# Two row halves as one 128-column stationary for the second half of each expert's w1

## The reference, cut to what matters

```python
def run_block(args):
    xblk, e = args
    hid = jax.nn.silu(xblk @ w1[e]) * (xblk @ w3[e])
    return hid @ w2[e]
...
y = jnp.zeros((T + 1, D), jnp.float32).at[slot_tok].add(yb.astype(jnp.float32) * slot_w[:, None])[:T]
```

## Time and profile before

| | |
|---|---|
| median of 3 runs | 1729.02 us (1728.03 to 3334.2) |
| profiled execution | 1730.86 us, its span 1729.0 us |
| PE matmul busy | 1625.4 us, 94% of the span |
| VectorE busy | 1100.1 us, 64% |
| ScalarE busy | 879.8 us, 51% |
| GpSimd busy | 631.2 us, 37% |
| DMA | 340.98 MB, mean 197 GB/s |
| mean granted clock | 0.976 |

### The profile page before, as it was taken

The page is one execution under the profiler, slowest core; times in us unless marked ns, Lnnn a source line. Parts: engine busy times, 40 slices in busy tenths (PEclk is TensorE's granted clock), DMA queues, the critical chain, the costliest instruction groups (busy, mean ns, idle before and its releaser), DMA issues.

```text
span 1729.0 us, 22131 instructions
## 1 busy us (share of the span) xinstructions
PE 1625.4 (94%) x7116; PEld 1220.4 (71%) x7116; DVE 1100.1 (64%) x1449; ACT 879.8 (51%) x1241; POOL 631.2 (37%) x373
## 2 busy tenths in 40 slices
PE   3899999999999999999989998995999999999996
PEld 3788888777878788778878887683666665665654
DVE  6776865371422448433576543336999999999986
ACT  4544533433222333234455334433877877877775
POOL 0578886333324335324464433110122222222221
PEclk9999999999999999999998999996999999999998
DMA  9343444143121153532223221256999999999993
GB/s 324 103 116 111 138 151 160 55 146 103 50 104 49 49 219 134 195 122 93 98 69 109 74 98 49 56 204 251 379 403 405 398 407 400 398 388 377 391 389 123
DMA packets 135424, 340.98 MB, mean 197 GB/s; under 512 B 14596, under 2 KB 66060, under 8 KB 110521
## 3 DMA queue, kind: packets, MB, share of 16 engines
q1 hardware_dynamic: 127938, 320.71, 49.8%
q0 software_dynamic: 5200, 8.41, 2.2%
q10 hardware_dynamic: 2215, 10.93, 1.6%
HBM read 329.78 MB, written 18.87 MB: 202 GB/s over the span
## 4 chain that ended last, share of the span: by engine, by line
PE 61%; DMA 17%; DVE 12%; issue 6%; ACT 3%; DVEq 1%; SPq 0%; POOLq 0%; ACTq 0%; POOL 0%
PE ps L768 17%; PE ps L769 17%; PE ps L770 17%; DMA ring<-in_w 16%; PE ps L740 5%; DVE parts L2388 3%; PE ps L750 2%; DVE act_parts L2388 2%; PE ps L1128 1%; DVE arena L2431 1%; PE ps L1015 1%; DMA ring<-in_w_ada 1%; DVE arena L2447 1%; DVE arena L2081 1%; ACT parts L1226 1%
## 5 line engine op out<-in xcount | busy, mean ns | idle before, releaser
L2502 POOL TENSOR_TENSOR parts<-ring,parts 128x1024 fp32r<-128x1024 f32 x172 | 426.0, 2482 | 620.2 <-ACT parts L1226 617.0
L1226 ACT CAST parts<-ring 128x1024 fp32r<-128x1024 f32 x174 | 180.5, 1048 | 363.3 <-PE ps L770 327.7
L768 PE MATMUL ps<-parts,act_parts 128*128 128x512 f32 (+2 forms) x832 | 327.4, 394 | 7.5 <-DVEq L1909 3.0
L769 PE MATMUL ps<-parts,act_parts 128*128 128x512 f32 (+2 forms) x832 | 322.5, 388 | 0.0
L770 PE MATMUL ps<-parts,act_parts 128*128 128x512 f32 (+2 forms) x832 | 322.4, 387 | 0.0
L768 PE MATMUL ps<-act_parts,parts 128*128 128x512 f32 x640 | 252.0, 394 | 5.0 <-DVEq L1814 5.0
L769 PE MATMUL ps<-act_parts,parts 128*128 128x512 f32 x640 | 249.7, 390 | 0.0
L770 PE MATMUL ps<-act_parts,parts 128*128 128x512 f32 x640 | 249.5, 390 | 0.0
L768 PEld LDWEIGHTS ps<-parts,act_parts 128*128 128x128 f32 (+1 forms) x832 | 150.4, 181 | 72.8 <-issue 32.5
L1601 ACT CAST parts<-ring 128x1024 fp32r<-128x1024 f32 x144 | 144.7, 1048 | 75.7 <-PE ps L770 70.2
L770 PEld LDWEIGHTS ps<-parts,act_parts 128*128 128x128 f32 (+1 forms) x832 | 150.3, 181 | 39.3
(11 more groups left out here) (295 smaller groups left out, 2502.8 us busy)
## 6 DMA issues: line engine op xcount, KB each, us to landing
arena<-in_w SPq DMA_DIRECT2D x96, 1024.0 KB, 13.2
ring<-in_w SPq DMA_DIRECT2D x96, 1024.0 KB, 14.8
ring<-in_w_in SPq DMA_DIRECT2D x30, 1024.0 KB, 7.3
ring<-in_w_in SPq DMA_DIRECT2D x34, 512.0 KB, 5.2
ring<-in_w_ada SPq DMA_DIRECT2D x12, 1024.0 KB, 10.4
ring<-in_w_ret_out SPq DMA_DIRECT2D x8, 1024.0 KB, 6.3
ring<-in_w_out SPq DMA_DIRECT2D x8, 1024.0 KB, 7.6
ring<-in_w_in SPq DMA_DIRECT2D x16, 256.0 KB, 4.1
```

The lines of the kernel that those rows point to most:

```text
L768: pe.matmul(o, lhs[1], rhs[0], start=start, stop=False)
L769: pe.matmul(o, lhs[0], rhs[1], start=False, stop=False)
L1226: act.copy(parts[:, g % 4, 0, :], ring[:, st.place(j), k * 1024:(k + 1) * 1024]).then_inc(dense_hi, 1)
L2502: pool.tensor_tensor(parts[:, g % 4, 1, :], ring[:, st.place(j), k * 1024:(k + 1) * 1024], parts[:, g % 4, 0, :].bitcast(F32), ALU.subtrac ...
```

## The change

Pieces 2 and 3 of w1 are multiplied as w3's are: `xgT[:, t]` with its 128 columns, two products in place of three. Bank 1 then has two row halves. So that all its 128 partitions are begun, the fp32 product of the first half starts with its fourth K tile as a stationary operand of 128 columns whose last 64 are zero (`last_rows`); the zeros are a fifth tile behind `xg_rows`, set once in the routing stage. ScalarE copies the low row half (`low_gate`), VectorE adds it to the high one in `silu_rows` and writes the sum to `t_h`, waits for its own result and releases bank 1; ScalarE applies Silu to `t_h` in place (`gate`), after the cast of piece 8; `hidden` waits for `silu_ready`. Two instructions that set a semaphore without waiters (`x_ready`) are removed.

```diff
@@ allocation and the routing stage
-        xg_rows = carve([KT // 2, SLOTS])
+        xg_rows = carve([KT // 2 + 1, SLOTS])
+        last_rows = xg_rows[:, KT // 2 - 1:, :].rearrange("p t n -> p (t n)")
...
+            own(dve.memset(xg_rows[:, KT // 2, :], 0.0))
@@ PE, up
-                for t in range(KT // 2):
-                    mm = pe.matmul(o[0:SLOTS, :], xg_rows[:, t, :], w1[:, t * FF:(t + 1) * FF], start=t == 0, stop=False)
+                t = KT // 2 - 1
+                pe.matmul(o, last_rows, w1[:, t * FF:(t + 1) * FF], start=True, stop=False)
+                for t in range(KT // 2 - 1):
+                    mm = pe.matmul(o[0:SLOTS, :], xg_rows[:, t, :], w1[:, t * FF:(t + 1) * FF], start=False, stop=False)
...
-                        if n < 4:
-                            mm = split_product(o[0:SLOTS, :], [xgT[:, t, h, :] for h in range(2)], [w[:, h, half] for h in range(2)],
-                                               t == 0, t == KT - 1)
-                        else:
-                            rows = xgT[:, t].rearrange("p h s -> p (h s)")
-                            pe.matmul(o, rows, w[:, 0, half], start=t == 0, stop=False)
-                            mm = pe.matmul(o, rows, w[:, 1, half], start=False, stop=t == KT - 1)
+                        rows = xgT[:, t].rearrange("p h s -> p (h s)")
+                        pe.matmul(o, rows, w[:, 0, half], start=t == 0, stop=False)
+                        mm = pe.matmul(o, rows, w[:, 1, half], start=False, stop=t == KT - 1)
@@ ScalarE
-            def gate(stage, i=0):
-                drained(stage, 1, act.activation(t_h[0:SLOTS, :], full(stage, 1, i)[0:SLOTS, :], ACT.Silu))
+            def low_gate(stage, i=0):
+                act.copy(up_low[0:SLOTS, :], full(stage, 1, i)[SLOTS:2 * SLOTS, :]).then_inc(up_low_ready, 1)
+
+            def gate(b):
+                act.wait_ge(gate_sum_ready, b + 1)
+                act.activation(t_h[0:SLOTS, :], t_h[0:SLOTS, :], ACT.Silu).then_inc(silu_ready, 1)
...
-                gate("moe", i)
+                low_gate("moe", i)
                 high(8, i, 1 - odd)
+                gate(b)
@@ VectorE
+            def silu_rows(stage, b, i=0):
+
+                dve.wait_ge(up_low_ready, b * 2 + 1)
+                ins = dve.tensor_tensor(t_h[0:SLOTS, :], full(stage, 1, i)[0:SLOTS, :], up_low[0:SLOTS, :], ALU.add)
+                ins.then_inc(gate_sum_ready, 1)
+                dve.wait_ge(gate_sum_ready, b + 1)
+                drained(stage, 1, dve.nop())
...
-                dve.wait_ge(bank_drained[st.place(1)], st.before(1, i) + 1)
+                dve.wait_ge(silu_ready, b + 1)
...
                     for n in (6, 7, 8, 9, 10, 11):
                         low(n, r * 20 + (14 + 10 * q + n), q if n < 8 else 1 - q)
+                        if n == 7:
+                            silu_rows("moe", b, r * 2 + (1 + q))
```

More of the change, by code:

```diff
@@ L446, in build @@
             "gates_stored", "gates_in", "gates_used", "merged_ready"))
-        ms_ready, rms_ready, x_ready = (sem(n) for n in ("ms_ready", "rms_ready", "x_ready"))
+        ms_ready, rms_ready = (sem(n) for n in ("ms_ready", "rms_ready"))
         x_rms_ready, in2_r_ready = sem("x_rms_ready"), sem("in2_r_ready")
@@ L475, in build @@
         conv_stored, conv_back = sem("conv_stored"), sem("conv_back")
-        block_w_ready, slot_w_ready, idx_out_ready = sem("block_w_ready"), sem("slot_w_ready"), sem("idx_out_ready")
+        block_w_ready, idx_out_ready = sem("block_w_ready"), sem("idx_out_ready")
         settled = sem("settled")
+        gate_sum_ready, silu_ready = sem("gate_sum_ready"), sem("silu_ready")
         out_done = sem("out_done")
@@ L1620, in high_rows @@
                 o = full(stage, k, i)
-                act.copy(xg_rows, o[:, 0:KT // 2 * SLOTS].rearrange("p (t n) -> p t n", t=KT // 2)).then_inc(xg_rows_ready, 1)
+                act.copy(xg_rows[:, 0:KT // 2, :], o[:, 0:KT // 2 * SLOTS].rearrange("p (t n) -> p t n", t=KT // 2)).then_inc(xg_rows_ready, 1)
                 act.copy(xgT[:, :, 0, :], o.rearrange("p (t n) -> p t n", t=KT)).then_inc(xgT_hi, 1)
-            def gate(stage, i=0):
-                drained(stage, 1, act.activation(t_h[0:SLOTS, :], full(stage, 1, i)[0:SLOTS, :], ACT.Silu))
+            def low_gate(stage, i=0):
[3 more added lines that the diff above has]
+                act.activation(t_h[0:SLOTS, :], t_h[0:SLOTS, :], ACT.Silu).then_inc(silu_ready, 1)
             def low_up(stage, i=0):
@@ L1638, in _ @@
             high(7, 0, 0, used=(up_used, 1))
-            gate("moe_first")
+            low_gate("moe_first")
+            gate(0)
             low_up("moe_first")
@@ L2016, in _ @@
                 dve.tensor_tensor(x[:, m, :], x[:, m, :] if m else x0_early, y_tok[:, m, :], ALU.add).then_inc(row_ready, 1)
-            dve.nop().then_inc(x_ready, 1)
             low_T("h2T", 6, TAPS + 3)
@@ L2436, in add_rows @@
                 dve.nop().then_inc(y_sum_ready, 1)
+            def silu_rows(stage, b, i=0):
[4 more added lines that the diff above has]
+                drained(stage, 1, dve.nop())
             def hidden(stage, b, i=0):
-                dve.wait_ge(up_low_ready, b + 1)
+                dve.wait_ge(up_low_ready, b * 2 + 2)
                 moe(dve.tensor_tensor(up_sum[0:SLOTS, :], full(stage, 2, i)[0:SLOTS, :], up_low[0:SLOTS, :], ALU.add))
@@ L2443, in hidden @@
                 drained(stage, 2, dve.nop())
-                st = banks[stage]
-                dve.wait_ge(bank_drained[st.place(1)], st.before(1, i) + 1)
+                dve.wait_ge(silu_ready, b + 1)
                 w = slot_w[0:SLOTS, b:b + 1] if isinstance(b, int) else slot_w[0:SLOTS, bass.ds(b, 1)]
@@ L2460, in _ @@
             drained("route", 7, dve.nop())
+            silu_rows("moe_first", 0)
             hidden("moe_first", 0)
@@ L2467, in _ @@
                 low(n, 4 + n, 1)
+            silu_rows("moe", 1)
             for n in (8, 9, 10, 11):
```

## The result

The changed kernel takes **1758.78 us** (median of 4 runs, 1756.79 to 1765.85) against 1729.73 us of the kernel before, run beside it: a ratio of 1.018, 95% interval 1.016 to 1.020. One of the four executions of before took 3334.2 us; it is not in the ratio, and without it the median of before is 1729.02. The forecast was 1760. The profiled execution took 1759.38 us, its span is 1757.5 us, 28.5 longer than before's 1729.0.

A forecast was written before the change was run, and what follows sets the result against it. VectorE was taken to bound 25 passes of 16.07 us, DMA the last five. 25 x 1.15 = 28.8, plus 1.7 and 0.3, gave 30.8 us more: 1760 us against the median, range 1748 to 1772.

The forecast's parts named there:

- rivals 4 (PE): Expert loop: PE sets the pace, so four fewer matmuls give 0.94 us a pass back, 1706 us; chance 0.03.
- 3 (DMA hides it): Expert loop: DMA sets the pace and VectorE's extra work fits into its time, 1729 to 1735 us; chance 0.06.
- The last five passes: End of expert loop: VectorE's 17.22 us a pass exceeds the 16.88 that DMA allows, 1.7 us more in all.
- The term of VectorE and ScalarE: Each loop pass: new add, its wait and piece 9 delayed behind Silu, 1.15 us more a pass.
- self-wait: VectorE's wait for its own add, from the add's end T to piece 8's start: 0.27 to 0.35 us.
- Silu's delay of piece 9: ScalarE does Silu before piece 9's cast, so VectorE starts piece 9 at T (the add's end) + 1.61 us.
- The lower bound, 0.94: Least extra per pass: add 0.67 plus self-wait 0.27 us, if piece 9's cast is in time.
- rival 1: Expert loop, cheaper: piece 9 not delayed, only add and self-wait count, 0.94 us a pass, 1754 us; chance 0.13.
- The upper, 1.5: Most extra per pass, in us, if ScalarE wakes slower or its later copies also come late.
- rival 2: Expert loop, dearer: something else late behind Silu, 1.5 us a pass, 1770 us; PE's clock might also fall; chance 0.18.
- PE's 0.94 us: Each pass: four fewer w1 matmuls save PE 0.94 us, which turns into waiting and gains nothing.
- blocks 0 and 1, +0.3: First two blocks: block 0 net zero, block 1's piece 9 some 0.25 us later; 0.3 us set for both.

The follow-up runs named there:

- e1: Kernel before with only PE's part of the change (8 matmuls for 12; low rows' product of pieces 2 and 3 left out of the result): 1729.25 us, 0.9996.
- e2: Kernel before plus one unread 64x512 VectorE add and a wait for its own result, between pieces 7 and 8: 1750.63 us, 1.0132.
- f1: Kernel before with VectorE's waits for itself filled with work already there, and hid_ready set by the multiply itself: 1727.12 us, 0.9993.
- f3: e1 with the fillings of f1 in VectorE's waits for itself: 1730.17 us, 1.0008.
- e3: Changed kernel with ScalarE's Silu moved behind the cast of piece 9: 1751.51 us, 1.0135.
- f2: Changed kernel with Silu behind piece 9's cast and VectorE's waits for itself filled, also the new add's with piece 8's subtraction: 1742.36 us, 1.0078.
- e7: Changed kernel with Silu behind piece 9's cast, block 0's add early and piece 11's subtraction on GpSimd: 1832.11 us, 1.0585.
- e5: Kernel before with piece 11's subtraction moved from VectorE to GpSimd in the loop: 1821.84 us, 1.0532.
- e4: Changed kernel with block 0's new add moved ahead of VectorE's copy of the slots' weights: 1756.37 us, 1.0166.
- e8: e5 with PE's part of the change alone (low rows' product of pieces 2 and 3 left out): 1820.28 us, 1.0518.
- e6: Changed kernel with piece 11's subtraction moved from VectorE to GpSimd: 1837.04 us, 1.0636.

## Why the prediction was right, step by step

**What bounds.** VectorE set the 25 passes, as the earlier trace rows said: `e1` shows that PE's matmuls are worth nothing, `e2` that VectorE's add costs in full. That refutes rivals 4 (PE) and 3 (DMA hides it). Rival 3 was nearer than its 0.06 sounds: DMA stands right below 16.07 (`f1`, `f3`). The prediction's case against it used SyncE's waits for PE and VectorE in 1250 to 1600 us and left out two more lines of that view:

```profile
SPq L653 <- DMA ring<-in_w: 59.1, 30, 3.6
SPq L653 <- DMA arena<-in_w: 38.5, 25, 3.8
```

In 1540 to 1640 us of the kernel before SyncE waits for DMA alone (69.6 us), well ahead of the 1600 that the prediction names, and the passes still take 16.07 up to the 27th block. The last five passes, DMA's at 16.88, became 17.23 each, and +1.75 us was measured for 1.7.

**The term of VectorE and ScalarE**, 1.15 a pass: 1.155 measured. Its parts, too: add 0.68 for 0.67; self-wait 0.23 for 0.27 to 0.35 (T to piece 8); Silu's delay of piece 9, 0.27 or 0.28, for 0.20 (1.61 less 1.14 and 0.27). So the self-wait was set a little high and the delay a little low. The lower bound, 0.94, and rival 1 belong to a case without that delay, which `e3` built: it took 0.88, below the bound, as its self-wait is 0.22 and not 0.27. The upper, 1.5, was not approached, since ScalarE's later copies stayed in time and the granted clock of the loop stayed at 1.00, which rival 2 had in doubt. The Trainium skill (VectorE: DVE Perf Modes, The DRAIN you can't avoid) says that a semaphore after each of a chain of VectorE operations costs nothing extra; by that `e2` would have lost the start-to-start time of the add alone, which is 0.61 us where nothing is awaited (1449.97 to 1450.58 in `f2`), and it lost 0.82: the trace does not agree.

**PE's 0.94 us** turned into waits for VectorE, as said. **Bandwidth**: 377 GB/s forecast, 380 and 383 measured.

**The step that was mis-sized** is blocks 0 and 1, +0.3. They took 3.7 us more. In block 0 ScalarE's copy of w3's low rows (L1632) stands behind Silu, Silu behind the add, and the add behind VectorE's wait for PE's routing product:

```profile
1197.74 0.22 DVE L2470 COPY arena<-ps 64x64 f32<-64x64 f32 x1 [4.28 <-PE ps L742]
1198.18 0.68 DVE L2446 TENSOR_TENSOR arena<-ps,arena 64x512 f32<-64x512 f32 x1 [0.22 <-DVE arena L2470]
1200.03 0.68 DVE L2454 TENSOR_TENSOR arena<-ps,arena 64x512 f32<-64x512 f32 x1 [1.17 <-ACT arena L1632]
```

The prediction counted the add and its wait there, and not the 1.17 us of waiting for ScalarE's copy. It also let PE's product come 0.94 us sooner; from the block's low rows to VectorE's copy of that product (L2470) it takes 13.22 us instead of 13.57, so it came 0.35 sooner. That makes 16.35 us instead of 14.85 from the block's low rows (L2422, L2417 before) to its multiply. Block 0 to block 1 takes 17.25 us instead of 15.07: PE comes out of 4.11 us without work at half clock. Stretches of the kernel after, columns as in the earlier trace rows:

```profile
1202.00:1204.00 2.00, 2.00 (x6) 0.84 (x5) 2.00 (x3) 2.00 (x3) 0.00 (x0) 0.50 0.04 10
1204.00:1206.00 2.00, 2.00 (x3) 0.52 (x3) 2.00 (x3) 1.88 (x3) 0.00 (x0) 0.50 0.00 0
1206.00:1208.00 2.00, 2.00 (x5) 0.43 (x3) 2.00 (x3) 0.00 (x0) 0.00 (x0) 0.93 0.00 0
```

Nothing of that is seen in the total, because the profiled execution of the changed kernel came to the experts 6.0 us sooner (the router's products start at 1151.53, and at 1157.53 before) through code that is the same: in two 10 us stretches from 1070 on, before's granted clock was 0.75 and 0.83 and after's 1.00. It is not the code: `e2`, before's code up to there, starts these products at 1151.07, and `e7`, the changed code, at 1157.18. The sum for the two profiled executions: multiply of block 0 4.47 us sooner (1205.34 to 1200.87), block 1 +2.18, 25 passes +28.9, last five +1.75: 28.4 of the 28.5 us. The change's own terms come to 1.50 + 2.18 + 28.9 + 1.75 = 34.3 us, and the early start gives 6.0 back. So the forecast's sum, 30.8, came out near the truth with 3.4 us missing in one term and 6.0 us the other way, from a difference between two executions that no reading of the code could give. The term of the 25 passes was right by its mechanism; that the total came within 1.2 us of the forecast is partly luck. The medians differ by 29.05, the four runs after by up to 9.1, so the 34.3 can't be tested on the total.

## What to carry to other kernels

Where several engines are 80 to 99% busy, look for the one whose only idle entries are its own: there an added operation costs its full length and its wait, and what is saved on the engines that it releases is worth nothing. Before moving an operation behind a wait, list what stands behind it in that queue (Silu ahead of a cast cost 0.28 us a pass; a subtraction ahead of GpSimd's gather, with VectorE slowed beside it, 3.2). Before freeing the bounding engine, ask what comes next: here the transfers took back all of it. Idle time on VectorE can be what GpSimd works in: filling it made an index copy of 0.18 us take 3.6 to 4.4 (`f2`). An idle entry behind instructions that otherwise overlap understates the wait by that overlap.

## What was unexpected in the hardware

**The clock at the loop's start.** PE's work for block 1 begins at a granted clock of 0.50 (1.2 GHz) in some kernels, for 4 to 6 us, and at 1.00 in others; from block 0 to block 1 it is then 16.6 to 17.9 us, and 15.0 to 15.1 otherwise. It sorts by two things. With PE's code of before and 2.2 to 2.3 us idle ahead of block 1 (before, `e5`, `f1`) the clock stays at 1.00. With that code and 2.91 us idle (`e2`) it falls, to 0.50 in the lowest stretch. With the changed PE code, which has four matmuls fewer in block 0, it falls after 2.2 to 2.3 us idle as well (`e1`, `e4`, `e7`, `e8`, `f3`), and after 4.1 (after, `e3`, `e6`, `f2`). So PE's half of the change, the half that was to save time, is enough for the 2 us of block 1: `e1` alone has 2.05 of them. The add alone, by its longer idle time, has 1.77 (`e2`). In the loop itself, with short waits spread over a pass, the clock of the kernel after stays at 1.00. These are single profiles of each; how the two things combine stays open, and it is not excluded that the moment of the idle time counts beside its length.

**VectorE and GpSimd side by side.** In `e5` VectorE's multiply of two SBUF operands takes 1.84 us in this pass instead of 0.74 while GpSimd subtracts, and four subtractions take 6.78 (three take 3.49 and one more adds 1.14, so 4.63 elsewhere):

```profile
1465.80 1.84 DVE L2447 SCALAR_TENSOR_TENSOR arena<-arena 64x512 f32<-64x512 f32 x1 [0.35 <-DVE arena L2441]
...
1479.51 6.78 DVE L2388 TENSOR_TENSOR parts<-ring,parts 128x1024 fp32r<-128x1024 f32 x4
```

```profile
1464.22 2.87 POOL L2570 TENSOR_TENSOR act_parts<-arena,act_parts 128x1024 fp32r<-128x1024 f32 x1 [6.39 <-ACT act_parts L1601]
...
1482.04 3.17 POOL L2570 TENSOR_TENSOR act_parts<-ring,act_parts 128x1024 fp32r<-128x1024 f32 x1 [3.76 <-ACT act_parts L1601]
```

The multiply begins at 1465.80 and GpSimd ends at 1467.09. The Trainium skill (SBUF — State Buffer, SBUF: two separate sides) says that such a pair takes turns at a shared port, each for its whole instruction. By that the multiply would end at 1467.09 + 0.74 = 1467.83; it ended at 1467.64, so the trace agrees within 0.2 us. GpSimd's long copies in `f2` fit it from the other side: each ends within 0.05 us of VectorE's last subtraction of two SBUF operands.

**Bandwidth.** 405 and 403 GB/s over the first 200 us of `f1`'s stretches and 392 and 388 over the next, with a share of 1.01 to 1.02 in all of them: what the queues deliver at that share falls by 4% within the loop. `f3` has 400 and 405, then 390 and 388, at the same shares. Why is open.
